# A two-block transformer stack: the dilated attention mixer of the last layer rewritten

## The chip, the cores and the metric

The kernel runs on one core of a Trainium2 chip. The metric is the device time of one execution, in microseconds. All data are float32; dense products use the fp32r form, attention uses plain float32 products.

## The reference, cut to what matters

256 tokens of width 1024 pass through a first block (two layers) and a second block (two layers). The change concerns the mixer of the second block's last layer:

```python
def rms_norm(x, gain):
    xf = x.astype(jnp.float32)
    y = xf * lax.rsqrt(jnp.mean(xf * xf, axis=-1, keepdims=True) + RMS_EPS)
    return (y * gain.astype(jnp.float32)).astype(x.dtype)
...
    # the mixer: p = h @ w_q, 768 columns for 12 dilated heads, 256 for 4 memory heads
    q_d = rms_norm(p[..., :DIL_WIDTH].reshape(B, S, 3, 4, 64), q_gain)
    for g, (window, dilation) in enumerate(((128, 1), (512, 4), (2048, 16))):
        table = rel_bias[:, 4 * g:4 * g + 4]
        o_g, l_g = dilated_group_attention(q_d[:, :, g], k_sh[:, :, g], v_sh[:, :, g], table, window, dilation)
    alpha = jax.nn.softmax(jnp.stack(lses, axis=2), axis=2)
    h_d = (outs * alpha[..., None]).reshape(B, S, DIL_WIDTH)
    h_m = memory_cross_attention(p[..., DIL_WIDTH:], mem_n, w_mem_kv, mq_gain, mk_gain)
    return jnp.concatenate([h_d, h_m], axis=-1) @ w_out
```

Each dilated head adds a bias that depends on the distance of query and key alone. Softmax over the three groups' log sums, times each group's own softmax, is one softmax over the three groups' scores together, and so the kernel computes it: for one head index and one tile of 128 queries, three groups of scores stand side by side. Memory attention has four heads and 256 keys; its queries and keys are normed per head too.

## The kernel before, in words

**Weights.** Every weight slab (128 rows by 8 by 128 columns, 512 KB) goes through a ring of RING = 7 slots: SyncE loads it (`wraw`) once the slab seven places ahead of it is `used`; ScalarE copies it to fp32r (`whi`, L1243, `hi_until`); VectorE subtracts to get the rest (`wlo`, L1906, `lo_until`). A product of a slab is 24 matmuls of 256 columns on TensorE (`products`, L518): high by high, low by high, high by low. ScalarE and VectorE convert LEAD = 4 slabs ahead (`ahead`). All matmuls are recorded at one line, L516.

**Order.** Each engine has a program of its own; queues run in order, and semaphores tie them. The stages are: two layers of the first block, then `ffn(4)`, `mixer2a`, `ffn(5)`, `shared_kv`, `ffn(6)`, `mixer2b`, `ffn(7)`. The change is in `mixer2b` and in `ffn(6)` ahead of it. In a mixer `weave` (L215) runs a main generator step by step, and after each step lets the side generators go on; `c.step` counts. Every engine weaves the same steps, so the order within a queue is written out by hand.

**mixer2b before.** Four slabs of queries are multiplied with the input as its columns come in (`head`), then the statistic of the norm is made. Then come the bias rows: `bias_table` (L2644) multiplies ones with one column of the bias table, TensorE multiplies this with the one-hot matrix `ohb` (33 by 512), so that all 128 output rows hold the same row of biases; ScalarE copies it (L1808) and writes it to memory (`scratch`); twelve times, with two buffers. GpSimd reads each back with a step of 511, so that row p is shifted by p (L509). Then `headnorms` (L617, L1364, L2091): one query slab at a time is taken with the row statistic (L2107), squared (L1379), its mean over each head made by a product with `mean64` into bank 7, rsqrt'ed by ScalarE (L1264, L1266) and one Newton step of VectorE (L1923, L1925, L1927), and multiplied in (L2115). The four slabs of `mkv`, memory keys and values, follow in the same way (`mem_kv`), with their input made there (L1604, L2394).

`dilated` goes beside it from step 4 on, a unit per step: scores of three groups; bias added (L2677); maximum (L2680), negated; exponential with its sum (L1832); reciprocal (L2684) and scaling of the whole row (L2686) on VectorE; 3 or 6 transposes (L1163); copies (L1841, L1843); products with V. There are eight units, alternately short (384 wide) and long (768 wide). Each waits for its exponential, scaling and transposes within a step or the next. `mem_attention` (L864, L1577, L2372) follows when all that is done, eight units of 256. Then eight output slabs (`bo`), an add to `hT` each (L2594), and the input of `ffn(7)` (L1279, L1937).

Of the kernel before, what the change touches and what calls it, by code (L numbers as in the profile page):

```python
# [14 lines left out]
P = 128  # L15
# [105 lines left out]
B_ORDER = [0, 2, 4, 1, 3, 5, 6, 7]  # L121
# [18 lines left out]
def weights(IN):  # L140
# [35 lines left out]
    def mem_kv(l):  # L176
        for s in range(4):
            cols(("mkv", l, s), IN["w_mem_kv_2"][l], s * P)

# [18 lines left out]
    for s in B_ORDER:  # L198
        cols(("bq", 0, s), IN["b_w_q_2"][0], s * P)
    mem_kv(1)  # L200
# [49 lines left out]
def program(nc, IN, out):  # L250
# [103 lines left out]
    bias = mb.take("bias", 12, T)  # L354
    hd = mb.pair("hd", 6, T)
    b_hm = mb.pair("b_hm", 2, T)
    b_km = mb.take("b_km", 2, T)
    b_vm = mb.take("b_vm", 2, 256)
    b_mp = mb.pair("b_mp", KD, T)
    SSb = [mb.take("ssb0", 3 * T), mb.take("ssb1", 3 * T)]  # L360
    PPb = [mb.take("ppb0", 3 * T), mb.take("ppb1", 3 * T)]
    PTb = [mb.take("ptb0", 3 * T), mb.take("ptb1", 3 * T)]
    ohb = mb.take("ohb", 1536)
# [61 lines left out]
    MEM_N = len(MEM_UNITS)  # L425

# [29 lines left out]
    def gpsimd_program():  # L456
# [55 lines left out]
    def tensor_program():  # L512
# [5 lines left out]
        def products(out_, u, w, x, n_k=KD, first=True, last=True, fill=None):  # L518

            E.wait_ge(S("hi"), u + 1)  # L520
            for k in range(n_k):
                if fill is not None:
                    E.wait_ge(S("xhi"), KD * fill + k + 1)
                mm(out_, w(k, 0), x(k, 0), first and k == 0, False)
            E.wait_ge(lo_ready[u % RING], u // RING + 1)
            for k in range(n_k):
                mm(out_, w(k, 1), x(k, 0), False, False)
            for k in range(n_k):
                if fill is not None:
                    E.wait_ge(S("xlo"), KD * fill + k + 1)  # L530
                m = mm(out_, w(k, 0), x(k, 1), False, last and k == n_k - 1)
            return m
# [84 lines left out]
        def headnorms(keys, x, before=lambda: None):  # L617

            for i in range(len(keys) + 1):
                if i < len(keys):  # L620
                    keys[i]()
                if i > 0:
                    E.wait_ge(S("hn_sq"), c.hn + 1)
                    if c.hn > 0:
                        E.wait_ge(S("hn_out"), c.hn)
                    before()
                    mm(bank[7][:, 0:T], C("mean64"), sqb[:, (i - 1) % 2, 0:T], True, True).then_inc(S("hn_ms"), 1)
                    c.hn += 1
                yield

# [7 lines left out]
        def ffn(F):  # L638
# [4 lines left out]
            if F == 5:  # L643
                wait_h(E, H_OF_FILL["f5"], HEAD - 1)
            head([(2 * j + z, P, AT[name, F, j]) for j in range(2) for z, name in enumerate("gu")], x, fill)
            for j in range(2, NF):
# [21 lines left out]
                if F == 4 and j == 12:  # L668
                    stat((0, T), 7)
            down(F, cols, n, a_hi, a_lo)  # L670
# [193 lines left out]
        def mem_attention(l, qm, km, vm, s_of, pp, pt):  # L864
            for i in range(MEM_N + 2):
                if i < MEM_N:
                    pair, tl, t0, n, h, hh = MEM_UNITS[i]
                    g = MEM_N * l + i
                    if i >= 2:
                        E.wait_ge(S("mem_e"), g - 1)  # L870
                    mm(bank[2 + i % 2][0:n, 0:T], qm[64 * hh:64 * hh + 64, pair, t0:t0 + n], km[64 * hh:64 * hh + 64, pair, :], True, True).then_inc(S("mem_s"), 1)
                if 0 <= i - 1 < MEM_N:
                    g = MEM_N * l + i - 1
                    z = (i - 1) % 2
                    E.wait_ge(S("mem_p"), g + 1)
                    if i - 1 >= 2:
                        E.wait_ge(S("mem_c"), g - 1)
                    for st in range(2):
                        m = E.transpose(bank[4 + z][:, st * P:st * P + P], pp[z][:, st * P:st * P + P], ident)
                    m.then_inc(S("mem_t"), 1)  # L880
                if 0 <= i - 2 < MEM_N:
                    pair, tl, t0, n, h, hh = MEM_UNITS[i - 2]
                    g = MEM_N * l + i - 2
                    E.wait_ge(S("mem_c"), g + 1)
                    if tl == 0 and hh == 0 and 2 * l + pair > 0:
                        E.wait_ge(S("mem_o"), 2 * l + pair)
                    for st in range(2):
                        m = mm(bank[6][64 * hh:64 * hh + 64, t0:t0 + n], vm[:, st, h * HD:h * HD + HD], pt[(i - 2) % 2][:, st * P:st * P + P], st == 0, st == 1)
                    m.then_inc(S("mem_pv"), 1)

        def mem_kv(l, mp, zb, before):
            xm = lambda k, part: mp[part][:, k, :]

            def before_turn():
                E.wait_ge(S("hn_out"), c.hn)
                before()
# [166 lines left out]
        def first_project(keys, i, x, fill):  # L1063
# [3 lines left out]
            elif i >= HEAD:  # L1067
                project(keys[i], x)
# [38 lines left out]
        def mixer2b():  # L1107
# [6 lines left out]
            def bias_rows():  # L1114
                E.wait_ge(S("onehot"), 16)
                for h in range(12):
                    g = h // 4
                    if h >= 2:
                        E.wait_ge(S("b_row_c"), h - 1)
# [1655 lines left out]
```

## Time and profile before

| | us |
| --- | --- |
| median of 3 runs | 2567.19 (2565.28 to 2571.98) |
| the profiled execution | 2574.36 |
| its span, first to last instruction | 2573.0 |
| last mixer, head's first product to last add (2185.91 to 2373.81) | 187.9 |
| mean granted clock of TensorE over the span | 0.967 |

The profile is of one execution. A busy time is the time in which an engine had an instruction of that kind under way; PE is TensorE, PEld its weight load, DVE VectorE, ACT ScalarE, POOL GpSimd, SP SyncE. The granted clock is a share of 2.4 GHz: 0.50 is the lower of two levels, 1.2 GHz. The DMA share is the mean busy share of the core's 16 transfer engines, and can pass 1 where packets overlap. In rows of groups, "idle before" is the engine's idle time just ahead of them, with what ended it.

### The profile page before, as it was taken

The numbers are of one execution on the slowest core, as the hardware profiler recorded it, in microseconds if no ns is written. First come the engines' busy times: TensorE is split into PE (matmuls) and PEld (weight loads), VectorE is DVE, ScalarE is ACT, GpSimd is POOL, SyncE is SP. The second block draws the span as 40 slices with busy tenths as digits, with TensorE's granted clock in tenths as the row PEclk, the third lists the DMA queues.
The fourth block names the chain that finished last, engine by engine and source line by source line (L and its number), as shares of the span: only waits on it lengthen the run. The fifth ranks groups of instructions, "written<-read, shape, count | busy, mean of one in ns | idle before, by whom it ended". The sixth has DMA issues, their size and how long they took to land.

```text
span 2573.0 us, 45875 instructions
## 1 busy us (share of the span) xinstructions
PE 2448.4 (95%) x18769; PEld 2322.9 (90%) x18769; DVE 1676.7 (65%) x3006; ACT 1246.6 (48%) x2099; POOL 33.6 (1%) x63
## 2 busy tenths in 40 slices
PE   7999999999999989999999998999999999769999
PEld 6999788899999977899999998989998999457999
DVE  5656777776575487778648846756656765455664
ACT  5444455554354445556445634645445644334542
POOL 2000000000000000000000000000000000000000
PEclk9999999999999999999999998989999999677999
DMA  7655433565465453346655653427655665412653
GB/s 193 174 179 141 117 91 109 141 182 176 148 178 175 158 132 99 99 137 189 189 183 162 183 176 102 119 58 191 185 184 157 180 189 171 127 41 83 180 181 140
DMA packets 589729, 385.85 MB, mean 150 GB/s; under 512 B 44587, under 2 KB 564111, under 8 KB 589392
## 3 DMA queue, kind: packets, MB, share of 16 engines
q1 hardware_dynamic: 585408, 374.00, 50.5%
q10 hardware_dynamic: 2336, 5.92, 0.6%
q0 software_dynamic: 1776, 2.98, 0.4%
q8 instruction: 150, 2.46, 0.4%
q14 instruction: 59, 0.48, 0.1%
HBM read 378.59 MB, written 4.19 MB: 149 GB/s over the span
## 4 chain that ended last, share of the span: by engine, by line
PE 87%; DVE 8%; ACT 2%; issue 1%; DMA 1%; ACTq 0%; DVEq 0%
PE bank L516 86%; DVE wlo L1906 2%; DVE ry L1925 1%; DVE ry L1923 1%; PE bank L825 0%; ACT whi L1243 0%; DVE smh L2357 0%; DVE rst L1927 0%; PE bank L601 0%; ACT rst L1264 0%; DMA xs<-in_x 0%; PE bank L1163 0%; ACT rst L1266 0%; DMA wraw<-in_w_ffn_gu 0%; DVE ssb L2677 0%
## 5 line engine op out<-in xcount | busy, mean ns | idle before, releaser
L1906 DVE TENSOR_TENSOR wlo<-wraw,whi 128x1024 fp32r<-128x1024 f32 (+2 forms) x723 | 866.7, 1205 | 290.7 <-ACT whi L1243 287.3
L1243 ACT ACTIVATE whi<-wraw 128x1024 fp32r<-128x1024 f32 (+2 forms) x723 | 746.9, 1042 | 596.5 <-DMA wraw<-in_w_ffn_gu 175.2
L516 PE MATMUL bank<-xhi,whi 128*128 128x256 f32 (+2 forms) x4024 | 606.6, 291 | 40.7 <-ACT xhi L1279 24.6
L516 PE MATMUL bank<-xhi,wlo 128*128 128x256 f32 (+2 forms) x4024 | 592.8, 287 | 11.4 <-DVE wlo L1906 11.4
L516 PEld LDWEIGHTS bank<-xhi,whi 128*128 128x128 f32 (+1 forms) x4024 | 535.4, 190 | 63.0 <-ACT xhi L1279 27.1
L516 PE MATMUL bank<-xlo,whi 128*128 128x256 f32 (+2 forms) x4024 | 581.4, 285 | 0.0
L516 PEld LDWEIGHTS bank<-xhi,wlo 128*128 128x128 f32 (+1 forms) x4024 | 535.5, 190 | 15.4 <-DVE wlo L1906 15.1
L516 PEld LDWEIGHTS bank<-xlo,whi 128*128 128x128 f32 (+1 forms) x4024 | 528.2, 188 | 0.2
L516 PE MATMUL bank<-act_hi,wlo 128*128 128x256 f32 (+1 forms) x1408 | 400.5, 284 | 0.0
L516 PE MATMUL bank<-act_lo,whi 128*128 128x256 f32 (+1 forms) x1408 | 400.1, 284 | 0.0
L516 PE MATMUL bank<-act_hi,whi 128*128 128x256 f32 (+1 forms) x1408 | 399.1, 283 | 0.0
L516 PEld LDWEIGHTS bank<-act_hi,whi 128*128 128x128 f32 x1408 | 266.1, 189 | 0.0
L516 PEld LDWEIGHTS bank<-act_lo,whi 128*128 128x128 f32 x1408 | 264.8, 188 | 0.0
L516 PEld LDWEIGHTS bank<-act_hi,wlo 128*128 128x128 f32 x1408 | 264.3, 188 | 0.0
L1988 DVE TENSOR_TENSOR su<-bank,rst 128x256 f32<-128x256 f32 (+1 forms) x176 | 75.4, 429 | 224.0 <-PE bank L516 224.0
L1355 ACT ACTIVATE act_hi<-su 128x256 fp32r<-128x256 f32 (+1 forms) x176 | 73.6, 418 | 67.9 <-DVE su L1993 66.0
L1279 ACT ACTIVATE xhi<-hT,gain 128x256 fp32r<-128x256 f32 (+1 forms) x104 | 52.4, 513 | 98.0 <-DVE hT L1959 53.5
L1351 ACT ACTIVATE sg<-sg 128x256 f32<-128x256 f32 (+1 forms) x176 | 72.6, 412 | 47.2 <-DVE sg L1988 47.0
L1997 DVE TENSOR_TENSOR act_lo<-su,act_hi 128x256 fp32r<-128x256 f32 (+1 forms) x176 | 74.9, 426 | 7.8 <-ACT act_hi L1355 7.8
L1988 DVE TENSOR_TENSOR sg<-bank,rst 128x256 f32<-128x256 f32 (+1 forms) x176 | 74.7, 425 | 7.9 <-PE bank L516 7.7
L1993 DVE TENSOR_TENSOR su<-su,sg 128x256 f32<-128x256 f32 (+1 forms) x176 | 74.9, 426 | 2.0 <-DVE su L1988 0.5
L1918 DVE TENSOR_TENSOR ssum<-ssum,sqb 128x256 f32<-128x256 f32 (+1 forms) x120 | 51.7, 431 | 12.4 <-ACT sqb L1259 5.4
(396 smaller groups left out, 1815.9 us busy)
## 6 DMA issues: line engine op xcount, KB each, us to landing
wraw<-in_w_ffn_gu SPq DMA_DIRECT2D x176, 512.0 KB, 3.9
wraw<-in_w_ffn_down SPq DMA_DIRECT2D x88, 512.0 KB, 3.2
wraw<-in_ffn_w_gate SPq DMA_DIRECT2D x88, 512.0 KB, 3.9
wraw<-in_ffn_w_up SPq DMA_DIRECT2D x88, 512.0 KB, 3.9
wraw<-in_ffn_w_down SPq DMA_DIRECT2D x88, 512.0 KB, 3.3
wraw<-in_w_in SPq DMA_DIRECT2D x80, 512.0 KB, 3.9
wraw<-in_a_w_in SPq DMA_DIRECT2D x24, 384.0 KB, 3.2
wraw<-in_w_out SPq DMA_DIRECT2D x16, 512.0 KB, 3.8
```

Source lines behind the costliest of these rows:

```text
L516: return E.matmul(out_, lhsT, rhs, start=first, stop=last, skip_group_check=True)
L1243: A.activation(flat(whi, u), flat(wraw, u), ACT.Copy).then_inc(S("hi"), 1)
L1279: A.activation(xh[:, k, cols[0]:cols[1]], hT[:, k, cols[0]:cols[1]], ACT.Copy, scale=fill_gain(name)(k)).then_inc(S("xhi"), 1)
L1351: A.activation(s_g[:, j % 2, 0:n], s_g[:, j % 2, 0:n], ACT.Silu).then_inc(S("silu"), 1)
L1355: A.activation(a_hi[:, j, 0:n], s_u[:, j % 2, 0:n], ACT.Copy).then_inc(S("act_hi"), 1)
L1906: V.tensor_tensor(flat(wlo, u), flat(wraw, u), flat(whi, u).bitcast(F32), ALU.subtract).then_inc(lo_ready[u % RING], 1)
L1918: V.tensor_tensor(ssum[:, 0:n], ssum[:, 0:n], sqb[:, k % 2, 0:n], ALU.add).then_inc(S("ssum"), 1)
L1923: own(V.scalar_tensor_tensor(u, src, eps, dst, ALU.add, ALU.mult))
L1925: own(V.scalar_tensor_tensor(u, u, -0.5, dst, ALU.mult, ALU.mult))
L1988: V.tensor_tensor((s_g, s_u)[z][:, j % 2, 0:n], bank[b][:, 0:n], rst[:, cols[0]:cols[1]], ALU.mult).then_inc(S("gu_free"), 1)
L1993: V.tensor_tensor(s_u[:, j % 2, 0:n], s_u[:, j % 2, 0:n], s_g[:, j % 2, 0:n], ALU.mult).then_inc(S("act_mul"), 1)
L1997: V.tensor_tensor(a_lo[:, j, 0:n], s_u[:, j % 2, 0:n], a_hi[:, j, 0:n].bitcast(F32), ALU.subtract).then_inc(S("act_lo"), 1)
```

## The change

- `b_mp` and the bias rows are made in `ffn(6)`: the memory's high and low parts at j = 12 to 19, and at j = 4, 6 and 8 one product each of four columns of the table with 512 columns of `ohb`, giving four rows. ScalarE copies them to `ohb`; GpSimd writes each row 128 times to `scratch`, reading its one partition again and again, and then reads the bias back as before. `bias` and `ohb` are placed behind the feed-forward's buffers.
- Norms are made in place, from six buffers of squares and two banks, without `headnorms`; the memory's slabs are woven between the query slabs.
- A unit spreads over four steps: scores, bias, maximum and exponential; reciprocal and a diagonal matrix with it on ScalarE; products of the exponentials' blocks with that diagonal, in place of scaling and transposing; products with V. Memory attention goes beside it from step 10 on, in the same way.
- The first six of eight parts of four output slabs are multiplied before memory attention is done. The output uses banks 0 to 7.

```diff
+B_HEAD = [("bq", 0, s) for s in (0, 2, 4, 1)]
+B_ORDER = [("bq", 0, 3), ("bq", 0, 5), ("mkv", 1, 0), ("bq", 0, 6), ("mkv", 1, 1), ("bq", 0, 7), ("mkv", 1, 2), ("mkv", 1, 3)]
+B_NORMS = (B_HEAD + B_ORDER)[0:10]
+B_NORM_AT, B_NORM_STEP = (2, 2, 3, 3, 4, 5, 6, 7, 8, 9), (2, 3, 3, 4, 4, 5, 6, 7, 8, 9)
+B_UNIT_STEP, B_MEM_STEP, B_TURN_STEP = 4, 10, 11
+B_IDLE, B_EARLY = 5, 4
+B_ROW_AT = (4, 6, 8)
...
@@ gpsimd_program @@
...
-        u = AT["d", 6, NF - 1]
+        u = AT["d", 5, NF - 1]
         G.wait_ge(S("used"), u + 1)
         G.dma_start(ohb[0:BUCKETS + 1, :], IN["onehot"]).then_inc(S("onehot"), 16)
+        for g in range(3):
+            G.wait_ge(S("b_row_c"), g + 1)
+            for q in range(4):
+                G.dma_start(IN["scratch"][4 * g + q:4 * g + q + 1], ohb[q:q + 1, 512 * g:512 * g + 512].unsqueeze(1).broadcast_to([1, P, 512])).then_inc(S("bias_out"), 16)
...
@@ tensor_program, ffn @@
+                if F == 6 and j in B_ROW_AT:
+                    g = B_ROW_AT.index(j)
...
+                        E.wait_ge(S("b_row_c"), g)
+                    mm(bank[6][0:4, :], tab[0:BUCKETS + 1, 4 * g:4 * g + 4], ohb[0:BUCKETS + 1, 512 * g:512 * g + 512], True, True).then_inc(S("b_row"), 1)
...
@@ tensor_program, mixer2b @@
+            def main():
+                head_projects(B_HEAD, x, FILL["b"])
+                stat(cols2, 7)
+                yield
+                for i, key in enumerate(B_ORDER, HEAD):
...
+                    if i >= HEAD + 2:
+                        E.wait_ge(S("evac"), c.proj - 1)
+                    c.proj += 1
+                    products(b_bank(i)[:, 0:T], AT[key], slab_cols(AT[key], 0, P), xm if key[0] == "mkv" else x).then_inc(S("used"), 1)
+                    yield
+                for _ in range(B_IDLE):
+                    yield
+
+                E.wait_ge(S("b_out"), 6)
+                for d in range(B_EARLY):
+                    u = AT["bo", 0, d]
+                    products(bank[d][:, 0:T], u, slab_cols(u, 0, P), xo, n_k=6, last=False)
+                    yield
...
+            def norms():
+                for n in range(len(B_NORMS)):
...
+                    E.wait_ge(S("hn_sq"), hn0 + n + 1)
+                    if n >= 2:
+                        E.wait_ge(S("hn_out"), hn0 + (n - 1 if n < 4 else n))
+                    mm(b_norm_bank(n), C("mean64"), bsq[:, n % 6, :], True, True).then_inc(S("hn_ms"), 1)
...
+                    if 0 <= n - 2 < B_UNITS_N:
+                        h, i, rows, t0, W = b_unit(n - 2)
+                        E.wait_ge(S("b_d"), n - 1)
...
+                            m = mm(o, PPb[(n - 2) % 3][:, q * P:q * P + P], dgb[(n - 2) % 2], True, True)
+                        m.then_inc(S("b_t"), 1)
...
+            weave(main(), [norms(), turns(), dilated(), memory()], c)
             E.wait_ge(S("mem_o"), 4)
...
+                if d < B_EARLY:
+                    products(bank[d][:, 0:T], u, slab_cols(u, 0, P), xo, n_k=2, first=False, k0=6).then_inc(S("used"), 1)
+                else:
+                    products(bank[d][:, 0:T], u, slab_cols(u, 0, P), xo).then_inc(S("used"), 1)
...
@@ scalar_program, mixer2b @@
+                stat(cols2, 7)
+                A.wait_ge(S("bias_out"), 16 * 12)
+                for n in range(HEAD):
+                    square(n)
+                yield
...
+                        A.wait_ge(S("b_r"), n)
+                        if n - 1 >= 2:
+                            A.wait_ge(S("b_t"), n - 2)
+                        A.activation(dgb[z], ident, ACT.Copy, scale=stat_a[:, 4 * z + 3:4 * z + 4]).then_inc(S("b_d"), 1)
...
@@ vector_program, mixer2b @@
+                    V.wait_ge(S("hn_rsq"), hn0 + n + 1)
+                    V.wait_ge(S("evac"), c.first + n + 1)
+                    rsqrt(bsq[:, n % 6, :], b_norm_bank(n), "hn_rs")
+                    V.wait_ge(S("hn_rs"), hn0 + n + 1)
+                    g = 75 if name == "mkv" else 76 if s < 6 else 73
+                    V.scalar_tensor_tensor(b_raw(n), b_raw(n), gain2[:, g:g + 1], bsq[:, n % 6, :], ALU.mult, ALU.mult).then_inc(S("hn_out"), 1)
...
+                    if 0 <= n - 1 < B_UNITS_N:
+                        z = (n - 1) % 2
+                        V.wait_ge(S("b_e"), n)
+                        V.reciprocal(stat_a[:, 4 * z + 3:4 * z + 4], stat_a[:, 4 * z + 2:4 * z + 3]).then_inc(S("b_r"), 1)
```

TensorE's `ffn(7)` also gets the wait for four finished columns of `hT` that `ffn(5)` has.

## Rows read from the trace of the kernel before

**Rows 1.** The page: busy time, share and instructions of each engine.

```profile
PE 2448.4 (95%) x18769; PEld 2322.9 (90%) x18769; DVE 1676.7 (65%) x3006; ACT 1246.6 (48%) x2099; POOL 33.6 (1%) x63
```

**Rows 2.** Busy time of each engine by stretch of the last mixer.

```profile
core 0: us, PE busy (x) PEld busy (x) DVE busy (x) ACT busy (x) POOL busy (x), PEclk, DMA share, GB/s
...
2200.00:2220.00 20.00, 19.00 (x24) 6.47 (x24) 3.80 (x14) 7.17 (x12) 0.00 (x0) 0.57 0.67 214
2220.00:2246.00 26.00, 12.48 (x48) 9.33 (x48) 15.07 (x34) 9.70 (x19) 6.42 (x12) 0.61 0.32 92
2246.00:2290.00 44.00, 31.93 (x160) 26.75 (x158) 22.93 (x55) 15.07 (x32) 0.00 (x0) 0.75 0.13 36
...
2323.00:2349.00 26.00, 21.68 (x78) 12.31 (x77) 11.25 (x37) 9.73 (x33) 0.00 (x0) 0.62 0.08 21
```

**Rows 3.** Chain that ended last: start us, length us, what, with instruction counts.

```profile
2185.91 11.65 PE bank L516 x93
...
2200.34 19.01 PE bank L516 x24
...
2348.56 25.23 PE bank L516 x192
2373.81 0.44 DVE hT L2594
```

**Rows 4.** The same chain in the shared keys and values, a stage before.

```profile
1951.69 11.64 PE bank L516 x93
...
1975.12 0.48 DVE k_sh L2635
```

**Rows 5.** Groups by line and form, 2183 to 2400 us: count, busy us, mean ns, idle before.

```profile
L1906 DVE TENSOR_TENSOR wlo<-wraw,whi 128x1024 fp32r<-128x1024 f32 x26 | 31.7, 1219 | 1.9 <-ACT whi L1243 1.8
L1243 ACT ACTIVATE whi<-wraw 128x1024 fp32r<-128x1024 f32 x26 | 27.2, 1050 | 0.3 <-DMA wraw<-in_b_w_out 0.2
...
L516 PE MATMUL bank<-ohb,rst 33*128 33x512 f32 x24 | 19.0, 968 | 2.8 <-DVE rst L2648 2.8
...
L1264 ACT ACTIVATE sqb<-bank,eps 128x256 f32<-128x256 f32 x10 | 4.6, 462 | 2.6 <-PE bank L516 2.6
...
L1925 DVE SCALAR_TENSOR_TENSOR ry<-ry,sqb 128x256 f32<-128x256 f32 x10 | 4.3, 425 | 0.3
...
L2680 DVE TENSOR_REDUCE stat_a<-ssb 128x1 f32<-128x768 f32 x4 | 3.8, 953 | 0.1
...
L1832 ACT ACTIVATE ppb<-ssb,stat_a 128x768 f32<-128x768 f32 x4 | 3.7, 936 | 16.4 <-DVE stat_a L2682 16.4
...
L2686 DVE TENSOR_SCALAR ppb<-ppb,stat_a 128x768 f32<-128x768 f32 x4 | 2.5, 620 | 0.1
...
L2684 DVE RECIPROCAL stat_a<-stat_a 128x1 f32<-128x1 f32 x8 | 1.3, 164 | 7.5 <-ACT ppb L1832 7.5
```

**Rows 6.** TensorE's instructions in order of time: start us, length us, form, count.

```profile
2301.12 0.85 PE L1163 MATMUL bank<-cst,ppb 128*128 128x128 f32 x6 [0.87 <-DVE ssb L2677]
...
2306.19 1.56 PE L516 MATMUL bank<-k_sh,b_q 64*128 64x256 f32 x6
...
2313.97 1.49 PE L1163 MATMUL bank<-cst,ppb 128*128 128x128 f32 x6
...
2319.25 1.52 PE L516 MATMUL bank<-ptb,v_sh 128*64 128x128 f32 x12
...
2335.57 1.12 PE L516 MATMUL bank<-ptb,b_vm 128*64 128x128 f32 x4
2336.62 1.22 PE L516 MATMUL bank<-b_km,b_q 64*128 64x256 f32 x2
```

**Rows 7.** Transfers from 2150 to 2420 us: queues, then size and time to landing.

```profile
q10 hardware_dynamic: 1728, 3.15, 3.1%
...
bias_scratch<-bias ACTq DMA_DIRECT2D x12, 256.0 KB, 2.0
```

**Rows 8.** Busy time by stretch, in the feed-forward ahead (columns as in rows 2).

```profile
2020.00:2040.00 20.00, 20.00 (x172) 20.00 (x171) 17.40 (x29) 12.86 (x19) 0.00 (x0) 1.00 0.65 188
```

More of the change, by code:

```diff
@@ L862, in mixer1 @@
                 products(bank[d][:, 0:out_cols[1] - out_cols[0]], u, slab_cols(u, 0, P), xin(out_cols)).then_inc(S("used"), 1)
[L864 to L896, printed above, removed]
-            E.wait_ge(S("mp_lo"), KD * (l + 1))
-            yield from headnorms([lambda s=s: project(("mkv", l, s), xm) for s in range(2)], xm, before)
-            yield from values([("mkv", l, s) for s in (2, 3)], xm, zb, TOK_TILES2, 7, before_turn)
         def mixer2a():
@@ L1123, in project_b @@
[L1123 to L1145 removed]
+            xm = lambda k, part: b_mp[part][:, k, :]
@@ L1146, in dilated @@
+            def dilated():
+                for n in range(B_UNITS_N + 3):
+                    while c.step < B_UNIT_STEP + n:
+                        yield
+                    if n < B_UNITS_N:
+                        h, i, rows, t0, W = b_unit(n)
+                        E.wait_ge(S("hn_out"), hn0 + (3, 6)[h // 2])
                         if n > 0:
                             E.wait_ge(S("b_sb"), n)
-                        if n >= 2:
-                            E.wait_ge(S("b_c"), n - 1)
@@ L1858, in mixer2b @@
+            weave(main(), [norms(), turns(), dilated(), memory()], c)
+            c.proj += 12
             for d in range(KD):
@@ new lines, in memory @@
+            def memory():
+                for i in range(MEM_N + 3):
+                    while c.step < B_MEM_STEP + i:
+                        yield
+                    if 0 <= i - 1 < MEM_N:
+                        z = (i - 1) % 2
+                        V.wait_ge(S("mem_e"), MEM_N + i)
+                        V.reciprocal(stat_b[:, 4 * z + 3:4 * z + 4], stat_b[:, 4 * z + 2:4 * z + 3]).then_inc(S("mem_r"), 1)
+                    if i < MEM_N:
+                        mx, nm = (stat_b[:, 4 * (i % 2) + y:4 * (i % 2) + y + 1] for y in range(2))
+                        V.wait_ge(S("mem_s"), MEM_N + i + 1)
+                        own(V.reduce_max(mx, bank[4][:, 0:T], AX_X))
+                        wait_own()
+                        V.tensor_scalar(nm, mx, -1.0, None, ALU.mult).then_inc(S("mem_nm"), 1)
+                    if 0 <= i - 3 < MEM_N:
+                        pair, tl, t0, n, h, hh = MEM_UNITS[i - 3]
+                        if tl == 1 and hh == 1:
+                            to_lo(b_hm[1][:, pair, :], bank[7][:, 0:T], b_hm[0][:, pair, :], "mem_oh", 2 + pair + 1).then_inc(S("mem_o"), 1)
```

566 lines of the change are left out of this document (271 added, 295 removed).

## The prediction, made before the changed kernel ran

> **What bounds the kernel now.** I read the page first. TensorE is busy 95% of the span, VectorE 65%, ScalarE 48% [rows 1], so outside the mixers only less TensorE work can help. The busy time by stretch then shows one place where that isn't so: from 2200 to 2349 us, the last mixer, TensorE's granted clock is 0.57, 0.61 and 0.62 in three of the stretches, and in the second it is busy for 12.5 of 26 us [rows 2]. In the dense feed-forward ahead it is busy all the time at clock 1.00, 172 products in 20 us, 0.116 us each [rows 8]. The chain gives the borders: the four head slabs end at 2197.56 (2185.91 + 11.65), the bias rows hold it for 19.01 us, the output slabs take the 25.23 us up to 2373.79, and the add of the last one starts at 2373.81 [rows 3]. Between head and that add lie 176.3 us. Of TensorE's work at the full clock I count: sixteen slabs of 24 products, 44.7 us, and attention and norms of some 30 us. So about 100 us of the 176 are waits, the bias rows and the half clock, and that is what the change goes at.
>
> **The bias rows.** Removed: twelve products of 512 columns (24 records of 968 ns [rows 5]), which are alone on the chain for 19.01 us [rows 3], with twelve table builds, twelve copies and twelve issues behind them. Added in the feed-forward: three products with the same 512 columns. Before, one costs 1.58 us (19.01 / 12), nearly all at the half clock; at the full clock I take half of a 1.7 us pace, 0.85 us, so 2.6 us for three, on the path because TensorE is full there. Bounds: nothing (four rows of output instead of 128) and 4.8 us. Their three copies, and the sixteen operations for the memory's high and low parts, are covered: VectorE is busy 17.4 and ScalarE 12.9 of 20 us in that stage's fullest stretch [rows 8], 0.5 us more in 5.6 us fits. Without that cover each would cost up to 0.5 us. GpSimd's queue now carries twelve more issues, with waits in front of them; behind these stand only the twelve reads of the bias, needed more than 150 us later.
>
> **From the head to the first unit.** The stage that computes keys and values already does what the new code does here: takes, four squares together, norm products behind a further projection. There the first norm ends 12.3 us after the head's end (1975.60 less 1963.33 [rows 4]); I take it over. Then, step by step, from [rows 5]: second norm 3.4 us (low part 1.2, take 0.4, norm of three operations of 0.425 and one of 0.49); third 1.8; fourth 6.5, because in TensorE's queue the fourth mean product, which waits for the second norm, stands ahead of the memory's first slab; that slab then runs mostly at the half clock after the idle time, 5.1 us, and VectorE's take of it stands ahead of the norm; fifth 3.4 (mean product 0.5, logarithm 0.46, exponential 0.42, norm 1.8, handovers); the first unit's adds and maximum 1.5. Sum 28.9 us. ScalarE's new wait ahead of the first square, for all twelve row writes, has every later weight conversion behind it; it costs nothing as long as the rows have been written 150 us before, and the whole delay if they haven't.
>
> **The five steps with both.** With a unit spread over four steps, what goes around is VectorE and ScalarE: exponential of the unit (0.94 and 0.19, or 0.80 in all for a short one), high part 1.05, square 0.41, logarithm and exponential 0.88, norm 1.8, reciprocal 0.16, three adds 0.7 or 1.1, maximum 0.55 or 0.95, negation 0.15; that is 6.8 and 7.3 us, and with some seven handovers of 0.05 us 7.4 on average [rows 5]. Beside it TensorE has 24 products (2.8), a mean (0.5), scores (0.8 or 1.5), products with V (0.8 or 1.45) and the turned blocks. At the full clock that is 6.6 us, under the 7.4. Five steps: 37.0 us. The turned blocks are dearer: six transposes take 0.85 us at 2301.12 [rows 6], while a product with the diagonal is of the form of those with V, 12 records in 1.52 us, 0.24 a block. That is 0.11 more for each of 52 blocks, 6 us of TensorE. In return scaling leaves VectorE (0.62 for a long unit [rows 5]) and the wait for it; the sixteen diagonals go to ScalarE, bounded by nothing and by 0.42 each, while VectorE adds and reduces, where ScalarE has nothing else but the copies. Where a norm's wait goes, the unit's maximum is what is late next.
>
> **Steps without projections.** In steps 10 to 14 only single-precision attention is left. TensorE's own sum at the full clock is 18 us. The memory stretch before shows such work at 1.2 GHz without a gap: at 2335.57 four records in 1.04 us, then two in 1.15 [rows 6], double the short ones above. So the stretch is 18 or 36 us; both levels are seen, and I take 24, nearer the first, because the gaps before it are under 1 us while the low clock of 2323 to 2349 followed longer ones. The last low parts of the dilated heads add 2.4. Four steps with three quarters of an output slab and a memory unit are 3.55 us each at full clock, 14.2, double at half; taken 17, as the dense products bring the clock back. The last memory unit's chain leaves 3 us bare. Then 120 products of 0.116 us, 14.0, where before there were 192 in 25.23 us. The first output slab is now freed only by its second part, and the eighth is loaded into its place; that one is needed 11 us later (2.8 for the four second parts, 8.4 for three slabs), and a load (twice the 2.0 us that 256 KB take [rows 7], an estimate), high part and low part take some 6. The new wait of the last feed-forward's head for four finished adds is met by then.
>
> **Sum.** 28.9 + 37.0 + 26.4 + 17.0 + 17.0 = 126.3 us against 176.3: 50.0 less, and 2.6 more ahead of it, so 47.4 less. The profiled execution took 2574.36 us (span 2573.0) and would take 2527; it is 7.2 us above the median of 2567.19, from which I forecast 2520. With every stretch at full clock the gain is 60 (2507); with the half clock in all of the middle it is 17 (2550).
>
> **Rival one: the rows' spreading holds the weights (slower).** Before, each row is written out from 128 partitions, 256 KB, landed in 2.0 us. Now each of the twelve writes reads one partition 128 times. The twelve before kept the transfer engines busy for 3.1% of 16 times 270 us, 134 us for 3.15 MB, so one engine moves 23.5 GB/s [rows 7]. If sixteen engines drawing on one partition get no more than one engine does, the twelve need 134 us, and the weights of the feed-forward, which take 0.65 of the engines at 188 GB/s [rows 8], stand behind them in the same engines. The ring of seven slabs has some five in hand (14 us), six more pass in between if the bytes alternate (17 us); TensorE loses 134 - 31 = 103 us, and the time is 2623. It decides from the point where the twelve take more than 78 us (31 + 47), below 40 GB/s. If they take under 31 us nothing is lost. For it: the engines' busy share and the bytes rise and fall together, so an engine seems to serve little else while a packet lasts. Against it: no row shows two queues held up, and the reads could be served side by side. The Trainium skill, "SBUF — State Buffer", section "Door 1: The DMA port swizzle", gives transfers that touch partitions 0 to 3 one port and 27.6 GB/s; by it the twelve would take 114 us and the time would be 2603. No transfer here of that size is from so few partitions, so the trace neither agrees nor disagrees. I give this rival 0.35.
>
> **Rival two: the clock stays low.** TensorE's busy time at 0.61 and 0.62 [rows 2] shows that attention can run through a stage at 1.2 GHz. If the waits of the first three steps let it fall and the mixed steps don't lift it, TensorE is the bound of each (9 instead of 7.4), steps 10 to 14 take 36, the four after 22, and the start 5 more. The gain is then 17, 2550. Against it: the 24-product slabs in each step, which before brought it to 0.75 on average even with 3 us of idle time a step [rows 2]. Chance 0.10.
>
> **Rival three: it doesn't do what it says.** Were the four steps of a unit still tied by a semaphore (the reciprocal waiting for an exponential queued behind a weight conversion), the steps would stay at their old 11 us (44 us for four from 2246 [rows 2]), 18 us more than I count, and the gain would be 29: 2538, inside the forecast's own range. I see the waits one step behind in the code, so it gets no chance of its own.
>
> **How the numbers follow.** The forecast has 0.55, with 2507 to 2550 as its own range. Below 0.3%, 8 us, a measurement of this kernel can't tell a change from none. Rival two is faster by 17 us, but worse start or weights could bring it near zero; with the milder part of rival one (twelve writes of 70 to 86 us) this gives 0.03 for the same. Faster 0.63, slower 0.34. The range must reach into rival one: up to 2600 it takes in its milder half (twelve writes of up to 111 us) and leaves out the rest, below 0.2.
>
> **What would show it.** Right: in the feed-forward, TensorE without idle time from 2020 on, transfers of the rows landed in a few us each; first norm 12 us after the head; mixed steps of 7 to 8 us; the last add some 125 us after the head's end. Wrong: waits for weight transfers in the feed-forward with the busy share of the transfer engines above 0.9 and GB/s far below 188 (rival one); a clock near 0.5 from the fifth step on (rival two).

## The result and the profile after

| | before | after |
| --- | --- | --- |
| median, us | 2569.59 (2565.28 to 2574.29) | 2603.53 (2602.77 to 2606.61) |
| span of the profiled execution, us | 2573.0 | 2601.5 |
| head of the shared keys and values to head of the last mixer | 234.2 | 327.1 |
| end of that mixer's head to its last add | 176.3 | 114.0 |

The kernel became slower: ratio 1.0133 with a 95% interval of 1.0114 to 1.0151, 33.9 us. That is small but clear of the noise. The forecast of 2520 has the wrong sign; rival one, which I had given 0.35, said 2623.

The page of after: busy time, and the chain by engine.

```profile
PE 2424.3 (93%) x18803; PEld 2313.6 (89%) x18803; DVE 1662.9 (64%) x2978; ACT 1244.9 (48%) x2106; POOL 39.8 (2%) x75
...
PE 82%; DVE 9%; DMA 4%; ACT 3%; issue 1%; SPq 1%; DVEq 0%; ACTq 0%
```

TensorE is busy 93% of the span where it was 95% [rows 1], and transfers are on the chain with 4%. The transfers of 2000 to 2250 us, with the feed-forward ahead of the mixer (the share is that of 16 engines in the stretch; the last number of the issue is us to landing):

```profile
q0 software_dynamic: 1536, 4.72, 44.6%
...
bias_scratch<-ohb POOLq DMA_DIRECT2D x12, 256.0 KB, 26.8
```

A row written from 128 partitions had landed in 2.0 us [rows 7]; one drawn 128 times from one partition lands in 26.8, as a median that includes the wait for the other writes of its group of four. In the first group they land 12.9, 22.5, 31.9 and 39.1 us after their issues, one some 9.5 us after the other. By the packets in the trace the three groups last 38.4, 39.4 and 38.4 us from the first packet to the last, 116 us in all for 3.15 MB, 27 GB/s. The weights get 11, 11 and 14 GB/s meanwhile. The busy time by stretch, columns as in [rows 2], in that feed-forward and then in the mixer:

```profile
2020.00:2040.00 20.00, 20.00 (x157) 18.01 (x156) 15.61 (x27) 10.91 (x17) 2.12 (x4) 1.00 0.75 142
2040.00:2060.00 20.00, 6.78 (x58) 6.57 (x56) 0.42 (x1) 0.00 (x0) 0.00 (x0) 0.78 0.96 28
2060.00:2080.00 20.00, 1.63 (x2) 0.09 (x2) 4.00 (x7) 4.63 (x8) 1.39 (x3) 0.50 0.99 140
2080.00:2100.00 20.00, 20.00 (x149) 19.84 (x149) 5.05 (x8) 2.78 (x4) 0.68 (x2) 0.87 0.99 36
2100.00:2120.00 20.00, 2.61 (x23) 2.40 (x21) 0.00 (x0) 0.00 (x0) 0.00 (x0) 0.65 0.91 50
...
2140.00:2160.00 20.00, 0.86 (x8) 0.65 (x6) 0.00 (x0) 0.00 (x0) 0.00 (x0) 0.58 0.99 39
...
2300.00:2320.00 20.00, 14.84 (x86) 12.60 (x87) 13.96 (x31) 7.52 (x16) 0.00 (x0) 0.83 0.20 57
2320.00:2340.00 20.00, 17.80 (x129) 15.35 (x128) 15.04 (x36) 10.90 (x23) 0.00 (x0) 1.00 0.28 79
2340.00:2360.00 20.00, 17.74 (x119) 14.23 (x118) 14.26 (x43) 12.16 (x34) 0.00 (x0) 1.00 0.10 27
```

Against 20.00 us of 20 at clock 1.00 and 188 GB/s before [rows 8], TensorE runs 6.78, 1.63, 2.61 and 0.86 us in four of the stretches. There the transfer engines are busy 0.91 to 0.99 and yet move 28, 50 and 39 GB/s in three of them; in the fourth, in which the first group of writes ends at 2072.8, 140. Who waits for what, between 1990 and 2290 us (total, times, longest):

```profile
ACT whi L1271 <- DMA wraw<-in_ffn_w_gate: 76.0, 5, 38.0
...
PE bank L557 <- ACT whi L1271: 48.8, 2, 27.5
ACT whi L1271 <- DMA wraw<-in_ffn_w_up: 43.8, 8, 36.2
```

ScalarE's conversions wait 76.0 and 43.8 us for weights; TensorE waits for ScalarE behind them. The chain gives the borders, the three longest waits between them, one mixed step in its main pieces and the end. "SPq" is time in which SyncE stood in the issue of a weight transfer; such an issue takes up to 26.3 us while the writes run, and before at most 2.0:

```profile
1949.64 11.66 PE bank L557 x93
...
2038.35 38.10 DMA wraw<-in_ffn_w_up
...
2102.62 16.76 SPq L472
...
2124.20 42.91 DMA wraw<-in_ffn_w_gate
...
2276.74 11.64 PE bank L557 x93
...
2315.54 0.56 DVE stat_a L2701
...
2322.07 0.96 DVE stat_a L2701
...
2324.27 0.45 ACT whi L1271
...
2325.13 0.40 ACT ohb L1790
...
2326.37 0.43 DVE ry L1964
...
2328.31 0.59 DVE ssb L2698 x3
...
2328.93 0.56 DVE stat_a L2701
...
2348.23 0.96 DVE stat_a L2701
...
2357.86 28.33 PE bank L557 x196
...
2387.11 0.99 PE bank L557 x6
...
2388.11 5.59 DMA wraw<-in_b_w_out
...
2395.70 1.14 DVE wlo L1947
...
2402.42 0.34 DVE hT L2584
```

From head to head the feed-forward and the stage before it grew by 92.9 us (2276.74 - 1949.64 = 327.1; before 2185.91 - 1951.69 = 234.2). The mixer itself, from 2288.38 to 2402.42, takes 114.0 us, 62.2 less than the 176.3 [rows 3], and 12.3 less than forecast. So the net loss is a gain with a larger loss ahead of it: +92.9 - 62.2 = 30.7, against 28.5 by the spans (the stage with the shared keys and values starts 2.1 us earlier).

### The profile page after: what moved, and what is told of

The parts are those of the page before. It is cut to its first block, busy times and chain, and to the rows that moved or that the text cites. A ratio compares the mean times of both kernels' runs of the same rounds, so it can differ in the third digit from the quotient of the medians.

```text
span 2601.5 us, 45910 instructions
## 1 busy us (share of the span) xinstructions
PE 2424.3 (93%) x18803; PEld 2313.6 (89%) x18803; DVE 1662.9 (64%) x2978; ACT 1244.9 (48%) x2106; POOL 39.8 (2%) x75
## 4 chain that ended last, share of the span: by engine, by line
PE 82%; DVE 9%; DMA 4%; ACT 3%; issue 1%; SPq 1%; DVEq 0%; ACTq 0%
PE bank L557 81%; DVE wlo L1947 3%; DMA wraw<-in_ffn_w_gate 2%; DMA wraw<-in_ffn_w_up 1%; SPq L472 1%; ACT whi L1271 1%; DVE ry L1966 1%; DMA wraw<-in_w_ffn_gu 1%; DVE ry L1964 1%; PE bank L857 0%; ACT xhi L1307 0%; DVE xlo L1978 0%; DVE smh L2375 0%; DVE rst L1968 0%; PE bank L639 0%
## 5 line engine op out<-in xcount | busy, mean ns | idle before, releaser
L557 PEld LDWEIGHTS bank<-xhi,wlo 128*128 128x128 f32 (+1 forms) x4024 | 536.7, 190 | 16.1 <-DVE wlo L1947 15.6
L1978 DVE SCALAR_TENSOR_TENSOR xlo<-hT,gain,xhi 128x256 fp32r<-128x256 f32 (+1 forms) x104 | 50.0, 488 | 16.7 <-ACT xhi L1307 16.7
```

The costliest lines, as they stand in the source:

```text
L557: return E.matmul(out_, lhsT, rhs, start=first, stop=last, skip_group_check=True)
L1978: V.scalar_tensor_tensor(xl[:, k, cols[0]:cols[1]], hT[:, k, cols[0]:cols[1]], fill_gain(name)(k), xh[:, k, cols[0]:cols[1]].bitcast(F32), ...
```

## The experiments

The theory is rival one: a write that draws on one partition is slow, whoever issues it, and holds the weights. Against it stand the new work in the feed-forward itself (product, copies, waits), GpSimd's queue, and the number of transfer engines that the writes take. Every run stands beside the kernel before on the same chip; one given without a ratio is a single run. Where such a run is called faster or slower than another, the distance is far above 0.3%; closer ones are called alike.

**The rows on 32 partitions.** The product gets a left side 128 columns wide (each of four table columns repeated 32 times by VectorE), so each row stands on 32 partitions and the same 256 KB are drawn from all of them.

```diff
+                    for q in range(4):
+                        V.tensor_scalar(rst2[0:BUCKETS + 1, P * (g % 2) + 32 * q:P * (g % 2) + 32 * q + 32], C("ones")[0:BUCKETS + 1, 0:32], tab[:, 4 * g + q:4 * g + q + 1], None, ALU.mult).then_inc(S("b_tab"), 1)
-                G.dma_start(IN["scratch"][4 * g + q:4 * g + q + 1], ohb[q:q + 1, 512 * g:512 * g + 512].unsqueeze(1).broadcast_to([1, P, 512]))
+                G.dma_start(IN["scratch"][4 * g + q].rearrange("(a p) u -> p a u", p=32), ohb[32 * q:32 * q + 32, 512 * g:512 * g + 512].unsqueeze(1).broadcast_to([32, P // 32, 512]))
```

> The changed kernel, but each product's lhsT holds each of its four table columns 32 times, so a row of biases stands on 32 partitions and each write reads 32 partitions 4 times each; bytes, packets and queue are the same. Theory one (sixteen engines draw on one partition and hold the weights): a write lands in 2 to 5 us instead of 27, the feed-forward loses at most 3 us against before, and the time is 2603.5 less about 88, so 2512 to 2518. Theory two (GpSimd's queue or its number of issues is slow): writes still take over 20 us and the time stays above 2590.

Measured: 2518.52 us (2514.72 to 2521.53) against 2573.72, ratio 0.9796 [0.9779, 0.9813]. Its transfers, 2000 to 2250 us:

```profile
q0 software_dynamic: 1536, 4.72, 6.8%
...
bias_scratch<-ohb POOLq DMA_DIRECT2D x12, 256.0 KB, 5.1
```

The landing falls from 26.8 to 5.1 us and the queue's share from 44.6% to 6.8%. By the ratios to before the kernel takes 3.3% less time than after, some 87 us, by an edit that changes above all where the bytes are read from. What is left over in the feed-forward is work: from the shared head to the mixer's head it takes 242.0 us, 7.8 more than before, where I had expected at most 3. The chain shows where:

```profile
2013.70 1.14 DVE wlo L1949
...
2018.44 0.59 DVE rst L2085 x4
```

VectorE is behind: each low part on the chain is followed by the feed-forward's own operations, and the four table operations (0.59 us) stand in front of TensorE's product. TensorE is busy for 2.55 us of the five from 2015 to 2020, and its granted clock is 0.66 in the five behind them.

**Control: one partition, all else the same.** The wide product and the tables stay; each write draws on one partition (0, 32, 64, 96) 128 times.

```diff
-ohb[32 * q:32 * q + 32, 512 * g:512 * g + 512].unsqueeze(1).broadcast_to([32, P // 32, 512])
+ohb[32 * q:32 * q + 1, 512 * g:512 * g + 512].unsqueeze(1).broadcast_to([1, P, 512])
```

> As rows32 in TensorE's and ScalarE's work, but each write reads one partition 128 times: partitions 0, 32, 64 and 96 instead of 0, 1, 2 and 3. Theory one: still near 27 us to landing and a time of 2595 to 2606, if the writes of a burst are served one after another. If they are served side by side and the limit belongs to a group of neighbouring partitions, the twelve take half as long and the time is near 2545. If it was the 128-partition product and copy that helped in rows32, this is as fast as rows32.

Measured: 2599.69 us, landing in 24.3 us, TensorE at 0.00 of 20 us between 2060 and 2080. So neither the tables nor the wide product, but the reading from one partition makes the loss.

**The writes issued by ScalarE.** The same writes, on another queue.

```diff
@@ gpsimd_program @@
-            G.wait_ge(S("b_row_c"), g + 1)
-            for q in range(4):
-                G.dma_start(IN["scratch"][4 * g + q:4 * g + q + 1], ...)
@@ scalar_program, ffn, behind the copy to ohb @@
+                    A.wait_ge(S("b_row_c"), g + 1)
+                    for q in range(4):
+                        A.dma_start(IN["scratch"][4 * g + q:4 * g + q + 1], ...)
```

> The changed kernel with its twelve one-partition writes issued by ScalarE instead of GpSimd, nothing else. Theory one: the reading side limits, so it stays slow: 20 us or more to landing, 2595 to 2610. Theory two (the queue that GpSimd feeds is slow): landed in a few us, below 2530.

Measured: 2593.04 us, 2 us below the range.

```profile
q10 hardware_dynamic: 1728, 3.15, 37.9%
q0 software_dynamic: 576, 1.57, 2.0%
...
bias_scratch<-ohb ACTq DMA_DIRECT2D x12, 256.0 KB, 27.8
```

It lands no sooner (27.8 us). Here the writes have queue q10 to themselves: 37.9% of 250 us is 94.8 us of all sixteen engines. The reads alone, on q0, are 2.0%; taken off the 44.6% of after, its writes took 106.5 us of all sixteen. These are the times in which engines were occupied, and some were idle meanwhile. From first packet to last the writes take 77.5 and 38.2 us here (the first two groups run together), 116 us in all as in after, 27 GB/s. GpSimd's queue isn't the cause.

**Fewer engines.** A write of 127 rows and one of the last row, which I thought would stay on one engine and leave the other fifteen to the weights; first from GpSimd's queue, then from ScalarE's.

```diff
-                G.dma_start(IN["scratch"][4 * g + q:4 * g + q + 1], ohb[q:q + 1, 512 * g:512 * g + 512].unsqueeze(1).broadcast_to([1, P, 512]))
+                G.dma_start(IN["scratch"][4 * g + q:4 * g + q + 1, 0:P - 1, :], ohb[q:q + 1, 512 * g:512 * g + 512].unsqueeze(1).broadcast_to([1, P - 1, 512]))
+                G.dma_start(IN["scratch"][4 * g + q:4 * g + q + 1, P - 1:P, :], ohb[q:q + 1, 512 * g:512 * g + 512].unsqueeze(1))
```

> The changed kernel with each write split into 127 rows and 1 row. 127 is prime, so the 127 rows should all go through one transfer engine, which still reads one partition at some 23.5 GB/s: the twelve take about as long as before, 115 to 135 us. Theory one with its second half (a slow packet holds its own engine, and through it the weights): fifteen engines are free and on the sixteenth a weight packet waits for one fast broadcast packet, not for one shared sixteen ways; a slab gets through in some 2.8 to 4 us, and the time falls to 2520 to 2560. If instead the partition's reads or the memory's writes as such hold the weights, the time stays near 2603.

Measured: 2608.32 us, and not confined: the transfer engines' share is 0.93 to 0.98 between 2040 and 2160 us, q0 takes 43.6%. This run tests nothing of its theory.

The same two writes with `A.dma_start`, in ScalarE's program behind the copy:

> one_engine again, with ScalarE issuing the twelve pairs of 127 rows and 1 row. GpSimd's queue spread the 127 rows over all engines in 4 KB pieces; the queue of ScalarE may keep them on one. If it does: packets of 2 KB take about 86 ns again instead of 1100, the twelve take 115 to 140 us in all, and the weights are held on one engine only: 2520 to 2560. If the rows are spread again: 2590 to 2610, as act_queue, and the question stays open.

Measured: 2615.49 us. A stretch (columns as in [rows 2]), and two pieces of the chain:

```profile
2140.00:2160.00 20.00, 0.00 (x0) 0.00 (x0) 0.00 (x0) 0.00 (x0) 0.00 (x0) 0.50 0.07 27
```

```profile
2048.08 13.04 ACTq L1373
...
2096.31 12.74 ACTq L1373
```

Now the share is 0.07, about one engine of sixteen. Over the feed-forward the writes' packets take 129.5 us of one engine for 3.15 MB, 24 GB/s: nearly as much as sixteen draw from one partition. Fifteen engines are free for the weights, but TensorE stands still all the same: ScalarE hangs in the issue of its own writes (13.04 and 12.74 us, "ACTq"), and the conversion of the weights is queued behind it. The time is far outside the 2520 to 2560 for this case: I had left out that a queue's issue can hold its engine. So no run shows what fifteen free engines would be worth.

**One edit later: the rows in another place.** Tables three steps ahead of the product and products at j = 7, 9, 11.

```diff
-B_ROW_AT = (4, 6, 8)
+B_ROW_AT = (7, 9, 11)
-                if F == 6 and j + 1 in B_ROW_AT:
+                if F == 6 and j + 3 in B_ROW_AT:
```

> rows32 with its three row products at j = 7, 9 and 11 of the feed-forward instead of 4, 6 and 8, and VectorE's table operations three steps ahead of the product instead of one. In rows32 TensorE waited some 3.4 us for the tables near 2016 us, VectorE being full there, and had a half-clock stretch after it. Theory one says nothing else of the rows is on the path: 4 to 6 us less than rows32, so 2512 to 2515. Rival: TensorE is held by the weights while the writes land, wherever they are: no change.

Measured: 2513.83 us (2510.64 to 2518.04) against 2567.62, ratio 0.9784 [0.9761, 0.9808]. The intervals of this and the first overlap; the trace shows 238.0 us from head to head in place of 242.0. Its median is the lowest of the study. Two stretches of its feed-forward and its borders:

```profile
2040.00:2060.00 20.00, 20.00 (x164) 19.11 (x163) 11.92 (x23) 9.28 (x14) 2.20 (x4) 1.00 0.73 212
2060.00:2080.00 20.00, 20.00 (x164) 19.11 (x163) 13.32 (x24) 9.59 (x15) 4.37 (x8) 1.00 0.94 261
```

```profile
1947.17 11.66 PE bank L558 x93
...
2185.13 11.66 PE bank L558 x93
...
2312.86 15.98 PE bank L558 x117
```

TensorE is busy throughout these stretches, at clock 1.00, with the rows' transfers beside the weights'. 127.7 us from the mixer's head to the next: 62.9 less than the 190.6 of before (2376.5 less 2185.91).

**The rows alone.** The kernel before with the rows made ahead in this form, and its old mixer (no interleaving, no diagonals). The buffers and the load of the one-hot matrix move with them, as in after.

```diff
@@ the kernel before, ffn(6), tensor_program @@
+                    mm(bank[6][:, :], rst2[0:BUCKETS + 1, P * (g % 2):P * (g % 2) + P], ohb[0:BUCKETS + 1, 512 * g:512 * g + 512], True, True)
@@ headnorms @@
-                if i == 0:
-                    bias_rows()
```

> The kernel before with only the bias rows moved, in the form of rows32_later: tables, three products, copies and writes in the feed-forward, and nothing of it in the mixer; norms, units, memory attention and output slabs are as before. Theory: the 19.0 us on the chain go and at most 3 come back: 2552 to 2558 against 2570 for before. The rest of what rows32_later gains, some 38 us, then belongs to the interleaving. Rival: without the rows the loads that they covered become the wait, and under 12 us are gained.

Measured: 2552.15 us (2548.89 to 2555.3) against 2567.62, ratio 0.9932 [0.991, 0.9955]. The mixer's head to the next head takes 170.7 us (before 190.6). Its first stretches, to be read against [rows 2]:

```profile
2194.00:2220.00 26.00, 11.06 (x44) 8.23 (x45) 16.33 (x38) 9.58 (x19) 0.00 (x0) 0.67 0.34 89
2220.00:2246.00 26.00, 20.09 (x117) 17.78 (x118) 14.32 (x31) 9.51 (x19) 0.00 (x0) 0.80 0.15 41
2246.00:2290.00 44.00, 30.63 (x150) 24.63 (x148) 23.50 (x58) 17.02 (x40) 0.00 (x0) 0.73 0.12 36
```

The low clock stays: 0.67, 0.80, 0.73. So by the ratios 0.7% come from the rows, made ahead and read from 32 partitions, and another 1.5% (some 38 us) from the rewritten mixer, whose clock in the same place is 0.83 and then 1.00 (after's rows of 2300 to 2360 us).

**The diagonals undone.** The last version with VectorE's scaling and ordinary transposes in place of the products with a diagonal.

```diff
-                            m = mm(o, PPb[(n - 2) % 3][:, q * P:q * P + P], dgb[(n - 2) % 2], True, True)
+                            m = E.transpose(o, PPb[(n - 2) % 3][:, q * P:q * P + P], ident)
-                        A.activation(dgb[z], ident, ACT.Copy, scale=stat_a[:, 4 * z + 3:4 * z + 4])
+                        V.tensor_scalar(PPb[(n - 1) % 3][:, 0:3 * W1], PPb[(n - 1) % 3][:, 0:3 * W1], stat_a[:, 4 * z + 3:4 * z + 4], None, ALU.mult)
```

> rows32_later with the diagonal undone: VectorE scales each row of exponentials (0.42, 0.62, 0.35 us) behind the reciprocal, TensorE transposes as before, ScalarE makes no diagonals. The memory and the dilated units keep their four steps. Theory: the five mixed steps, bound by ScalarE and VectorE in turn, get 0.5 us longer each (2.6 us in all), and TensorE gets 5.7 us of work less, of which the half that lies in steps 10 to 18 is on the path: the two cancel, within 3 us of rows32_later. Rival: the diagonal is what gives the new mixer its speed; then this is over 8 us slower.

Measured: 2514.43 us (2510.68 to 2518.47) against 2567.62, ratio 0.9786 [0.9759, 0.9814]; head to head 128.2 us against 127.7. No difference that these runs can tell: the diagonal is worth nothing here, in either direction.

**How many partitions, and which.** Each row on n partitions, four new forms between the first experiment and its control:

```diff
-ohb[32 * q:32 * q + 1, ...].unsqueeze(1).broadcast_to([1, P, 512])
+ohb[32 * q:32 * q + n, ...].unsqueeze(1).broadcast_to([n, P // n, 512])
```

For the fourth row of the table the slice is `ohb[32 * q:32 * q + 32:8, ...]`. With the two ends (the third column is from the packets in the traces, first to last of each of the three groups; the kernel before took 2570 to 2575 us on the chips of these runs):

| partitions of a row | median landing, us | a group of four writes, us | time, us |
| --- | --- | --- | --- |
| 1 | 24.3 | 35.4, 36.7, 33.3 | 2599.69 |
| 2 neighbours | 14.7 | 25.5, 27.7, 24.9 | 2561.28 |
| 4 neighbours | 21.0 | 21.4, 21.3, 22.1 | 2559.18 |
| 4, eight apart | 7.1 | 7.9, 7.4, 8.6 | 2527.54 |
| 16 neighbours | 7.5 | 8.9, 10.2, 10.3 | 2526.11 |
| 32 neighbours | 5.1 | 5.2, 6.5, 7.3 | 2518.52 |

> The kernel after, with each of the twelve rows held on four neighbouring partitions (32q to 32q+3) and each write reading every one of them 32 times. Theory A (the write is slow because one stretch of neighbouring partitions gives 26 to 30 GB/s, whatever partition of it is read): nothing changes: the writes land in 24 to 27 us, the weights are held as in the kernel after, 2590 to 2610 us. Theory B (the limit belongs to a single partition): the same 256 KB come from four of them, so that a write lands in about 7 to 9 us and the time is 2525 to 2550 us.

> The same with the four partitions of a row eight apart (32q, 32q+8, 32q+16, 32q+24). Theories A and B both expect a rate about four times that of one partition: a write lands in 7 to 10 us, 2525 to 2550 us. Only if the slowness were that of a write with few, long source rows as such (a third theory: the number of different rows read, not where they lie) would the pair agree with each other at something between 2540 and 2600 us. What tells A from B is the distance of this run from the one with neighbouring partitions.

The transfers of the two, four neighbours first:

```profile
q0 software_dynamic: 3840, 4.74, 24.2%
...
bias_scratch<-ohb POOLq DMA_DIRECT2D x12, 256.0 KB, 21.0
```

```profile
q0 software_dynamic: 3840, 4.74, 8.0%
...
bias_scratch<-ohb POOLq DMA_DIRECT2D x12, 256.0 KB, 7.1
```

A group is 1.05 MB, so four neighbours give 48 to 49 GB/s and four others 123 to 143, where one partition gave 27 in after and 28 to 32 in the control. The four that lie eight apart came out as expected. For the four neighbours neither theory's range was met: they are faster than one partition by a factor of 1.5 to 1.8, and not by 4. (The 27.5% in the next expectation is a share of 220 us; of 250 us it is the 24.2% shown.)

> The kernel after, with each row on two neighbouring partitions (32q, 32q+1), each read 64 times. Four neighbouring ones gave about 56 GB/s, one gives 28 to 30: by landing times 21.0 and 26.8 us, and by the share of the transfer engines 27.5% against 44.6%. Theory C (every partition gives up to 28 GB/s and four neighbours share a second limit of 56): two neighbours give 56 already, so landings of about 21 us and 2555 to 2565 us, like the run with four neighbours. Theory D (neighbours in pairs share what one gives, and the second pair brings the doubling): nothing changes against one partition: landings of 24 to 27 us and 2595 to 2610 us.

> The same with sixteen neighbouring partitions (32q to 32q+15), each read 8 times. If four neighbours share 56 GB/s and the next four have their own, sixteen give about 220 GB/s, as the four partitions eight apart did (landing 7.1 us, 2527.5 us): landings of 6 to 8 us and 2515 to 2530 us. If the limit of 56 belonged to a longer stretch of neighbours, the landings stay above 15 us and the time above 2545 us.

What tells these runs apart is the landing of the four writes of a group. The first group of after, of two, of four and of sixteen neighbours, in this order:

```profile
DMA to landing us min/median/max: 12.9/27.2/39.1
...
DMA to landing us min/median/max: 4.1/13.8/26.1
...
DMA to landing us min/median/max: 3.7/21.3/22.0
...
DMA to landing us min/median/max: 4.6/7.7/10.3
```

From one partition, and from sixteen, the writes land one after another at even distances. With two neighbours, six of the twelve land after 3.3 to 6.3 us and six after 23.1 to 27.5: the median of 14.7 lies between them and is no write's landing. All twelve count up one semaphore, and on this queue the trace has sixteen 4-byte packets for each transfer; a count of another write, from an engine with little to carry, can so pass for a landing. Only the last landing of a group is sure: 26 to 28 us for two neighbours, 21 to 23 for four. So two are not better than four, and the time that theory C gave for two fits. Sixteen came out as expected. With two neighbours some 7 engines are busy with the writes' packets at a time, with four 13 to 14. That looks as if each partition of each row had an engine of its own; it is also why the queue's share of the sixteen engines (15.6% for two, 24.2% for four) doesn't give a rate.

The last three of four neighbours' writes land within 2.3 us of each other. So, as I read it, the four writes of a group ran side by side, and their 48 to 49 GB/s come from sixteen partitions in four places, 32 apart, and not from four neighbours. Theory A, that one stretch of four neighbours gives no more than one of its partitions, is therefore not refuted: two such limits at work at once would give 54. Sixteen neighbours, written one row after another, give 101 to 118 GB/s, about four times one stretch. A limit of some 27 GB/s for each single partition doesn't fit: two neighbours, eight partitions read side by side, would give far more than the 38 to 43 measured. No run has a write from four neighbours alone, so the size of the limit of one stretch stays open.

## Why the prediction was wrong

- **The step that failed** is the one on ScalarE's wait for the row writes and on GpSimd's queue: it costed them at nothing as long as the rows are written in time. The rows were written in time; it was the weights that weren't. Rival one named this, with its place and the waits that would show it, and I gave it 0.35. The argument against it, that sixteen engines may be served side by side by one partition, was the one that fell: 27 GB/s against the 23.5 that [rows 7] gave for one engine. Had I weighed it by that row alone, "sixteen draw no more than one", it would have been the likelier case.
- **Its price.** The rival counted 134 us of writes less 31 us in reserve, a loss of 103. Measured: 116 us of writes, and a loss of 92.9 less the rows' own work. No run shows that work for after's own narrow product; with 3.7, from the last version with 32 partitions, 89 us are lost. So the reserve was some 27 us where I had 31: the rival's sum was nearly right, and too high mainly in the time of the writes. The Trainium skill, "SBUF — State Buffer", section "Door 1: The DMA port swizzle", gives 27.6 GB/s for partitions 0 to 3, by which I had 114 us; one partition measured 27 GB/s and the twelve 116 us here, so the trace agrees. That section's table puts partitions 0 to 3 and 32 to 35 on one port and 64 to 67 and 96 to 99 on another; the four neighbours' writes drew on these two, and their 48 to 49 GB/s don't contradict it. That its 2603 matches the median to 1 us is partly chance: it counted the loss 6 us too small and the mixer 12 us too slow.
- **Bias rows.** 19.0 us less was right: 19.9 measured, 190.6 to 170.7, in the run with the rows alone. The 2.6 added measured 3.7 with the wide tables in their later place, 7.8 in the first: VectorE's cover was thinner than the 17.4 of 20 us had let me think.
- **From the head to the first maximum**: 28.9 forecast, 27.7 measured (2288.38 to 2316.10). The first norm ends 12.2 us after the head's end, where I had taken over 12.3.
- **The five mixed steps**: 37.0 forecast, 33.1 measured (2316.10 to 2349.19), 6.6 each. In the step shown VectorE's and ScalarE's operations follow each other nearly without a gap, as I had counted them; the steps are shorter than my list because the weight conversion stands only partly on their chain (0.45 at 2324.27, where I had put 1.05; 0.77 to 0.95 in the others).
- **Steps 10 to 14 and the four early slabs**: 46.4 forecast with the last memory unit, 37.9 measured (2349.19 to 2387.11). TensorE is on the chain alone for 28.33 us with 196 matmuls, at clock 1.00. The fall to the half clock, for which I had put 24 us between 18 and 36 and 17.0 in place of 14.2, did not come: after the mixed steps TensorE had no long idle time, and the granted clock stayed. With that, rival two falls as well (0.83 in the first stretch of the mixer, then 1.00), and rival three with 6.6 us a step.
- **The output slabs**: 14.0 forecast, 15.3 measured. The eighth slab's load into the freed slot took 5.59 us and is on the chain, but its low part is done by 2396.84, 8.7 us after the first slab's end: more than the 6 I had estimated, within the 11 counted. VectorE, with low parts and adds in a row from 2395.70 on, ends 0.9 us after TensorE.
- **Sum.** 27.7 + 33.1 + 37.9 + 15.3 = 114.0 us against 126.3. With its transfers cured the change gives 2513.83 us, 53.8 less than the before of its chip, where the forecast had 47.4; in the traces the changed stages take 59.2 less (62.9 less 3.7). So the rest of the sum held within 12 us, too slow in three terms of four, and the one term that decided was the one put at nothing. The largest miss in the mixer, 8.5 us, is the stretch for which I had put in the lower clock.
- **The diagonals.** The 6 us of TensorE and the 0.62 us less of VectorE per unit were both put in; the run without them shows no difference.

## What to carry to other kernels

A transfer has a source as well as a size: before a row is spread by reading it again and again, count what the source partitions give, and compare with how long the other transfers can be held. 3.15 MB that occupy the sixteen engines for 8 us from 128 partitions occupy them for 106 from one, and what else is queued on these waits. Make the row on 32 partitions by a wider product and let the transfer repeat it four times only. Another queue did not help, and a single engine fed by ScalarE held ScalarE instead. And where several writes count on one semaphore, look at when the last one lands and not at the median.

## What the runs showed of the hardware

- One partition gives 27 GB/s to sixteen engines (3.15 MB in 116 us, on either queue; 28 to 32 with the rows on partitions 0, 32, 64 and 96), and 24 to a single one. Groups of four writes ran at 38 to 43 GB/s from two neighbours per row, 48 to 49 from four, 101 to 118 from sixteen, 123 to 143 from four partitions eight apart and 144 to 202 from 32 neighbours, with the weights beside them.
- While sixteen engines draw on one partition they are occupied (busy share 0.99 at 36 GB/s, 2080 to 2100 us), and the weights, on another queue, get 11 to 14 GB/s.
- A write of 127 rows issued by GpSimd went to all engines (share 0.93 to 0.98 between 2040 and 2160 us); the same one issued by ScalarE to about one (0.07).
- ScalarE, issuing such writes behind unfinished ones of its own, stood in the issue for up to 12.7 and 13.0 us at a time, with all that is queued behind it. SyncE stood for up to 26.3 us in the issue of a weight transfer in after; before, for at most 2.0 (2000 to 2250 us in both).
